# Query weights of the last two heads loaded as 120 and 8 rows in place of 128, on one core of a Trainium2

## What is computed

```
q = (xt @ w_query).reshape(T, PEER_HEADS, 2, PEER_DHALF)      # 8 heads, 256 columns each
s = einsum('thpd,pkd->thpk', q, sub_keys)
# per token and head: the 16 best of the product keys -> idx, gate
u = u_tab[idx];  act = gelu(einsum('thkd,td->thk', u, x))
out = einsum('thk,thkd->td', gate * act, v_tab[idx])
```

## Time and profile before

| | before |
|---|---|
| median of three runs | 2157.96 us |
| the profiled execution's own time | 2158.62 us |
| its span, first to last instruction | 2156.9 us |
| TensorE busy | 1883.4 us, 87% |
| VectorE busy | 1481.6 us, 69% |
| ScalarE busy | 685.3 us, 32% |
| GpSimd busy | 626.2 us, 29% |
| moved by DMA | 713.12 MB, 331 GB/s over the span |
| granted TensorE clock, mean | 0.975 |

### The profile page before, as it was taken

One profiled execution on the slowest core, in us unless ns is written; L12 is line 12 of the kernel. 1 busy time (PEld: TensorE's weight loads), 2 busy tenths in 40 slices (PEclk: granted clock), 3 DMA queues, 4 the chain that ended last, 5 costly groups with the idle time before them and its releaser, 6 DMA issues.

```text
span 2156.9 us, 21972 instructions
## 1 busy us (share of the span) xinstructions
PE 1883.4 (87%) x6340; PEld 1094.0 (51%) x6340; DVE 1481.6 (69%) x4053; ACT 685.3 (32%) x1905; POOL 626.2 (29%) x608
## 2 busy tenths in 40 slices
PE   4999999988878888877799999998889878889776
PEld 3677777654434434433267777775434334334332
DVE  6676687776766766766637676777766766766774
ACT  1222332233333333333322322241333333333332
POOL 4000000154444444345300000003444344344342
PEclk9999999999999999999999999999999999999989
DMA  9855563299999999999976544336999999999996
GB/s 365 331 186 198 216 224 125 88 418 422 421 422 421 421 421 421 420 414 420 411 289 247 199 181 159 127 111 268 421 421 421 421 421 421 422 419 420 418 416 258
DMA packets 118818, 713.12 MB, mean 331 GB/s; under 512 B 13104, under 2 KB 17456, under 8 KB 51120
## 3 DMA queue, kind: packets, MB, share of 16 engines
q0 software_dynamic: 73728, 536.90, 60.0%
q1 hardware_dynamic: 44976, 174.97, 21.6%
HBM read 710.78 MB, written 1.05 MB: 330 GB/s over the span
## 4 chain that ended last, share of the span: by engine, by line
PE 48%; DMA 27%; DVE 13%; issue 4%; POOL 3%; ACT 3%; SPq 2%; DVEq 0%; POOLq 0%; ACTq 0%
DMA wall<-in_peer_uv,idx 25%; PE PS L1193 13%; PE PS L944 11%; PE PS L949 9%; DVE wall L1258 5%; PE PS L954 5%; PE PS L1167 4%; POOL wall L622 3%; PE PS L1133 1%; ACT M L822 1%; PE PS L991 1%; PE PS L915 1%; DVE pos L1743 1%; ACT wgt L815 1%; PE PS L964 1%
## 5 line engine op out<-in xcount | busy, mean ns | idle before, releaser
L1193 PE MATMUL PS<-wall,M 128*128 128x512 f32 x2032 | 958.0, 620 | 217.1 <-ACT M L822 216.7
L1258 DVE CUSTOM_DVE_ANT_0 wall<-wall,tok 128x1024 f32<-128x1024 f32 x512 | 604.4, 1222 | 360.7 <-DMA wall<-in_peer_uv,idx 360.7
L622 POOL DMA_INDIRECT wall<-in_peer_uv,idx x512 | 567.6, 1109 | 721.2 <-PE PS L1193 350.5
L1193 PEld LDWEIGHTS PS<-wall,M 128*128 128x128 f32 x2032 | 385.0, 197 | 751.3 <-issue 412.8
L808 ACT ACTIVATE dg<-dg 128x2 f32<-128x2 f32 x254 | 51.6, 203 | 767.0 <-DVE dg L1258 767.0
L944 PE MATMUL PS<-hT,wall 128*128 128x256 f32 x1120 | 247.9, 380 | 1.7 <-DMA wall<-in_w_in 1.7
L944 PEld LDWEIGHTS PS<-hT,wall 128*128 128x128 f32 x1120 | 211.6, 190 | 32.0 <-issue 2.1
L949 PE MATMUL PS<-wall,hT 128*128 128x512 f32 x512 | 224.7, 592 | 0.2 <-ACT M L691 0.2
L564 POOL TENSOR_SCALAR rsb<-ms 128x4 f32<-128x4 f32 (+2 forms) x22 | 5.6, 253 | 747.8 <-DVE ms L1258 746.5
L822 ACT ACTIVATE M<-turn,wgt 128x128 f32<-128x128 f32 x508 | 176.1, 394 | 24.1 <-ACT wgt L815 0.7
L949 PEld LDWEIGHTS PS<-wall,hT 128*128 128x128 f32 x512 | 96.1, 190 | 109.3 <-issue 108.5
(11 more groups left out here) (279 smaller groups left out, 1870.1 us busy)
## 6 DMA issues: line engine op xcount, KB each, us to landing
wall<-in_w_in SPq DMA_DIRECT2D x112, 704.0 KB, 9.8
braw<-in_ada_rows SPq DMA_DIRECT2D x72, 512.0 KB, 4.2
wall<-in_w_out SPq DMA_DIRECT2D x2, 4096.0 KB, 14.5
wall<-in_peer_uv,idx POOLq DMA_INDIRECT x512, 15.2
wall<-in_ada_rows SPq DMA_DIRECT2D x6, 1024.0 KB, 12.3
wall<-in_w_in SPq DMA_DIRECT2D x16, 384.0 KB, 11.2
mix<-in_peer_w_query SPq DMA_DIRECT2D x6, 1024.0 KB, 6.7
wall<-in_w_in SPq DMA_DIRECT2D x16, 320.0 KB, 9.1
```

The source lines that it names most:

```text
L622: nc.gpsimd.indirect_dma_start(out=pair_rows[b][s], out_offset=None, in_=uv_rows, in_offset=bass.IndirectOffsetOnAxis(ap=idx[i % 2][:, k:k ...
L1193: ins = mm(bank(B_ACC + 2 * t + hf), diag[:, b, s, :], pair_rows[b][s][:, D + hf * 512:D + (hf + 1) * 512], start=(i == FIRST_TILE[t] and ...
L1258: return v.tensor_tensor_reduce(out=o, in0=a, in1=b, scale=1.0, scalar=0.0, op0=ALU.mult, op1=ALU.add, accum_out=acc)
```

## The change

The loads of heads 6 and 7 are made in two DMAs each, rows 0 to 119 and rows 120 to 127, both counted on the same semaphore, so that `s_r[0]` and `s_r[1]` rise by 48 in a layer. The waits on them are adapted. 120 rows can be dealt out as eight rows to each of fifteen DMA engines, and eight rows as one to each of eight.

```diff
+MOST = 120
...
+            def load_late_wq(l, h, done):
+
+                for rows in (slice(0, MOST), slice(MOST, P)):
+                    sp.dma_start(wq[h][rows], peer_w_query[l, h, rows]).then_inc(done, 16)
...
                 sp.wait_ge(s_chunk, HEADS * l + 2)
-                load_wq(l, HEADS - 2, s_r[0])
-                load_wq(l, HEADS - 1, s_r[1])
+                load_late_wq(l, HEADS - 2, s_r[0])
+                load_late_wq(l, HEADS - 1, s_r[1])
...
-                pe.wait_ge(s_r[1], 32 * l + 16)
+                pe.wait_ge(s_r[1], 48 * l + 16)
...
-                pe.wait_ge(s_r[0], 32 * l + 16)
+                pe.wait_ge(s_r[0], 48 * l + 16)
...
-                        pe.wait_ge(s_r[h - (HEADS - 2)], 32 * l + 32)
+                        pe.wait_ge(s_r[h - (HEADS - 2)], 48 * l + 48)
```

## The result

The changed kernel takes 2177.03 us in the median of four runs (2175.61 to 2177.82), the kernel before in the same session 2159.47 us (2156.13 to 2162.40). The ratio is 1.0083, with a 95% interval of 1.0071 to 1.0095: **slower by 17.6 us**, where 9.8 us less were forecast. The profiled execution took 2177.24 us. Its span is 2175.5 us, 18.6 us more than that of before.

The account below looks back on a forecast made before the run. It took each expert stage as bound by DMA transfers, its end set by one late engine. Sparing that engine 16 rows a layer gains 9.7 to 9.9 us, taken as 9.8: 2157.96 - 9.8 = 2148.2 us, 8-in-10 range 2146.5 to 2159.5.

Parts of the forecast that it names:

- the price of a packet: Loads of heads 6 and 7: an 8 KB packet stays at 0.311 us; extra cost taken as 0, at most 1.9 us.
- The spared engine is the late one: Expert stages: the engine relieved of 16 rows a layer is the one finishing last; with gain arriving, chance 0.52.
- An engine's rows can be handed to others: Split loads: one engine is spared 4.97 us a layer, eight engines get two more rows, 0.62 us; bytes unchanged.
- the likeliest case: Both expert stages: the spared engine is late and the gain arrives, 9.8 us, giving 2148.2 us; chance 0.52.
- The head start is kept: Expert stage: the engine relieved at 465 us never runs dry, keeping about 5 us; partly lost, about 2153 us, chance 0.08.
- The stage is bound by its transfers, and one of sixteen sets the end: Expert stages: one engine ends 5.3 and 5.6 us behind the next; sparing its 16 rows gains up to 4.97 us a layer.
- The dealing, the issues and the waits: Split loads: eight rows to fifteen engines, one to eight, 302 packets; at most 0.9 us of later issues, hidden; no wait added.
- the slower one, eight engines with all the rows: Rival: the 120 rows go to eight engines, 15 each, 9.9 us slower if one is late, 2167.9 us; chance 0.05.
- Dearer packets: Rival: split-load packets cost 0.06 us more on a late engine, 1.9 us for 32 rows; chance 0.02.

Follow-up runs that it names:

- e8: The kernel before, plus late in each expert stage 16 additional 8 KB rows for each of engines 0 to 3, to their own partitions: 2170.13 us, ratio 1.0047.
- e11: Changed kernel, but only partitions 0 to 15 and 32 to 47 of heads 6 and 7 loaded, by four-row DMAs stepping 4 partitions: 2159.14 us, ratio 0.9997.
- e12: The kernel before, plus late in each expert stage 16 additional rows for each of engines 0 and 1, to their own partitions: 2157.78 us, ratio 1.0003.
- e13: Against e12: the same late extra rows on engines 0 and 1, but written to partitions 8 to 15 and 40 to 47: 2168.97 us, ratio 1.0044.
- e10: The kernel before without loading heads 6 and 7 at all (queries use the tiles' old contents): 2149.51 us, ratio 0.9958.
- e3: Changed kernel, but only rows 0 to 63 of heads 6 and 7 loaded, by eight DMAs of eight rows 4 partitions apart: 2158.90 us, ratio 0.9998.
- e7: The kernel before, plus late in each expert stage 16 additional 8 KB rows for each of engines 0 to 7, to their own partitions: 2169.28 us, ratio 1.0045.
- e6: The kernel before, with heads 0 and 1, loaded when no gather runs, split into 120 and 8 rows; heads 6 and 7 whole: 2158.97 us, ratio 0.9999.
- e5: Changed kernel, but heads 6 and 7 split into rows 0 to 63 and 64 to 127 in place of 120 and 8: 2172.45 us, ratio 1.0060.

## Why the prediction was wrong

**The step that failed** is the price of a packet: "it cannot be cheaper than the 0.311 us [...] dearer by the spread of a full step, it would be 5.93 / 16 = 0.371 us [...] I take 0". It measured 0.54 us, and not for the 32 rows of one engine alone but in layer 0 for some 600 packets on all sixteen, the gathers' among them. The term was 0, at most 1.9 us, and had to be about 18. The reason given, that gather packets run at full speed although their rows "also come from anywhere", took the source for the destination: a gather reads from anywhere, but writes 128 partitions in the usual division. Nothing in the trace of before shows a row that goes to a group of partitions through another engine, and a full step's spread, which comes from an instruction fetch, is no bound for that.

**The spared engine is the late one:** wrong. e8, e11 and e12 leave the late one at engine 2 or 3 by the map; the fifteen lowest-numbered engines include both. The argument that a fixed duty belongs to an end of the row was as weak as it said.

**An engine's rows can be handed to others:** this was assumed without a word. In e13 rows for the late set cost 10.1 us although engines 0 and 1 carried them, which had carried as many to their own partitions for nothing. So it is doubtful that even the likeliest case would have brought its 9.8 us; no run spares the late engine alone.

**The head start is kept:** in part. e10 spares every engine at 465 us and the whole 10.1 us arrive. But in e3, where eight engines have nothing of the load, the share falls to 0.86 within 10 us: those engines run dry. A share of 1.01 before said only that no engine was far enough ahead to run dry. For a late engine spared alone it was not measured.

**The stage is bound by its transfers, and one of sixteen sets the end:** right. 0.311 us for a row gives 9.95 us for 32 rows; e10 gained 10.1 us, and e7 and e8 lost 10.5 and 11.3. The alone time of the earlier trace rows is there after the change as well.

**The dealing, the issues and the waits:** right. There are 302 packets, the count for fifteen and eight engines; SP's issues take 1.40 us in place of 0.76, and nothing waits for them; head 6's first matmul moves from 825.3 to 833.3 us with the stage, no wait in front of it.

**The rivals:** the slower one, eight engines with all the rows at 2167.9 us, named a wrong mechanism. "Dearer packets" had a chance of 0.02 and a size of 1.9 us: the right mechanism, mis-sized tenfold. The text's own bound, wrong above 2153 us, was passed by 24 us.

## What to carry to other kernels

Where other transfers run beside it, load all 128 partitions in one DMA, or in DMAs whose rows step by four within 32 partitions, as e3 does, so that each row arrives through the engine that also serves its group in the other transfers. In this kernel every load of fewer partitions in succession slowed the gathers beside it and cost 8 to 18 us. Before rows are moved from one DMA engine to another, ask which partitions they go to, and not only how many packets each engine has. And read the DMA share and the GB/s side by side: here a full share with half the rate was a conflict over partitions, and a fall of both was engines without work.

## What the runs showed of the hardware that was not expected

- A row of 8 KB took 0.54 us in place of 0.31 where two streams with different divisions met, with all sixteen engines shown as busy, and 0.59 in place of 0.38 for one such load alone (e6).
- For four loads, two DMAs of 64 rows each in place of one of 128 cost 13.7 us in this kernel (e5). The Trainium skill ("SBUF — State Buffer", section "Can I just issue two DMAs to hit both halves?") says that two such transfers serialize, measured at only 6% more than a single one; here the split is a loss, and one for the transfers beside it too.
- 16 rows more in a layer on each engine of the late set cost 5 to 6 us a layer when its own engines carried them (e7, e8) and 5 us when others did (e13); 16 rows each on engines 0 and 1 for their own partitions cost nothing (e12).
- Rows that came through another engine took 0.32 us themselves, and the gathered rows beside them 0.37 us in place of 0.32 (e13). The transfers that were in the right place bore the cost.
- The lateness lies with partitions 8 to 15 and 40 to 47, engine 2 or 3 by the map; the table in "DMA: Bandwidth & Descriptors" of the Trainium skill, section "Latency and other measured facts", calls engines 7 and 15 usually slower, and no run here shows that. Why it lies there, whether the instruction fetches have a part in it, which of the two engines it is, and whether it is the same in another program, stays open.
